# Feed-forward part of a decoder trunk: up products of two steps in turn, PSUM halves in turn in the down part, token sums in pieces, fewer products for the sample rows

## Chip, cores and metric

One Trainium2 chip, one of its cores. The metric is device time in microseconds (us) of one execution of the whole program; lower is better. PE is TensorE, DVE VectorE, ACT ScalarE, POOL GpSimd, SP SyncE, whose queue issues all the DMAs spoken of here.

## What is computed

The reference is a decoder layer (a mixer, then a squared-ReLU MLP) over 2048 prompt tokens and 8 sample tokens, in float32. The change touches only the MLP and the last norm:

```
x = x + ffn(rmsnorm(x, norm_ffn_g), w_up, w_down)      # x: 2048 + 8 rows of 1024
def ffn(h, w_up, w_down):                              # w_up 1024 x 4096, w_down 4096 x 1024
    return square(relu(h @ w_up)) @ w_down
y = rmsnorm(x, norm_f_g)
```

## The kernel before

The program projects, mixes (until about 1018 us of the profile) and then runs `ffn` (L1806), the only part that differs. Every matrix product is split by Strassen's scheme in Winograd's form: a 2x2 block product is made of 7 products k = 0..6 of sums of quarters. Each operand of a product is split in a high and a low part (`..._cut`, index 0 and 1), and `three_pass` (L114) issues three matmuls for each pair of 128-row pieces: L119, L120, L121.

**Up part.** 48 steps u (3 token blocks of 688 columns, 16 pairs of weight column blocks each), 7 products a step. A product is 4 pieces x 3 passes = 12 matmuls of 128x344. `SEQ` (L1762) is the order of all 336 products (a position in it is a tick); from step 2 on it is step by step, k = 0..6. `product(u, k)` on PE accumulates k = 0, 2, 4, 6 in `bank_a(u)` and k = 1, 3, 5 in `bank_b(u)`; three pairs of banks go round with u. Since a bank goes on being used, its sum so far has to be read out between products: k = 2 waits for ACT's copy of k = 0 (`copy_part`, L2256), k = 3 for DVE's `sum_part` of k = 1 (L2415), k = 4 for the copy of k = 2, k = 5 for the copy of k = 3, k = 6 for the sum of k = 4. `square_z` (ACT, L2263 and L2267) makes relu and square into `z`, which `store_z` (SP) writes to DRAM, both halves behind each other.

Weights: SP's `load_up(u)` brings 1 MB into one of two rooms `up_raw`; POOL's `sum_up(u)` makes four sums (L2091, L2093, L2096, L2100) into `wsum`; ACT cuts the high part (`w_cut_hi`, L2218), DVE the low one (`w_cut_lo`, L2375). Both run `LEAD` = 4 ticks ahead of PE and write `wc[:, k]`, one room for each k. The order on ACT at a tick is: cut of tick + 4, then the copy or the square of this tick, then what belongs to a turn or a block; on DVE: cut of tick + 4, `sum_part`, `scale_later`, `move_later`, `h_cut_lo`.

Tokens: the first block is turned at the start. The other rows are turned during the first steps: at 12 ticks `TURN_AT` (16 + 5i) PE transposes 128 rows (L2539), which DVE has scaled two ticks before (`scale_later`, L2409), and ACT and DVE move them out for a store. At the last step of a block (`u % PAIRS == 15`) `h_cut_hi` and `h_cut_lo` (L2236, L2379) cut the next block's tokens; POOL has made that block's four sums before, all in one go (`sum_h`, L2110; 128x1376 each), behind `sum_up(12)` and `sum_up(20)`, waiting for the block's load (`load_h`, L1967).

**Down part.** 16 chunks m of tokens and weight group g = m // 2, 7 products k each, `down(m, k)`. A product is 4 column pieces j x 2 x 3 = 24 matmuls of 128x512 into 4 banks: banks 0..3 for even k, 4..7 for odd k (`dbank`). DVE adds them into `acc` in two halves (`add`, L2441, 128x1024). `A_BEFORE`, `B_BEFORE` give the product whose adds a product waits for. ACT and DVE cut chunk parts (`z_cut_hi`, `z_cut_lo` L2420) two products ahead, and the weights of the next group over 7 products around each odd-to-even chunk change (`dn_cut_lo`, L2424); POOL makes the sums (L2131 to L2166). After each even chunk `sample(g)` multiplies the 8 sample rows: 10 pairs of a 32-column and a 64-column stationary operand, 128x512 each (L2605, L2607).

## Time and profile before

| | us |
|---|---|
| time before, median of 3 runs | 2510.64 (2510.34 to 2511.41) |
| the profiled execution, its own time | 2505.51 |
| its span, first to last instruction | 2503.8 |
| PE busy | 2337.5 (93%) |
| PE weight load busy | 2120.9 (85%) |
| DVE busy | 1622.3 (65%) |
| ACT busy | 986.6 (39%) |
| POOL busy | 796.4 (32%) |
| share of PE in the chain that ended last | 38% |

The profile is one execution. The page gives busy time by engine, a strip of 40 slices with the clock granted to TensorE, the chain of work that ended last, and the costliest groups of instructions. The end of a matmul is modelled, so PE's busy share says little; the distance from one matmul's start to the next one's says more. An idle time in square brackets stands in front of the instruction that ended it, with what released it.

### The profile page before, as it was taken

How to read it: one execution, taken by the hardware profiler on the slowest of the kernel's cores; microseconds unless marked ns; L12 is line 12 of the kernel's file. 1: busy time of each engine (PE TensorE's matmuls, PEld its weight loads, DVE VectorE, ACT ScalarE, POOL GpSimd, SP SyncE). 2: the span in 40 equal slices, each digit the busy share in tenths (PEclk: the TensorE clock that was granted, in tenths of full speed). 3: DMA queues.
4: the chain of work that ended last, by engine and by line, in shares of the span. 5: the costliest groups of instructions: out<-in, count | busy, mean ns of one | idle time of the engine just before them, and what ended most of it. 6: DMA issues, size and time to landing. Idle time of an engine off the chain costs nothing.

```text
span 2503.8 us, 34076 instructions
## 1 busy us (share of the span) xinstructions
PE 2337.5 (93%) x12740; PEld 2120.9 (85%) x12740; DVE 1622.3 (65%) x2317; ACT 986.6 (39%) x1959; POOL 796.4 (32%) x639
## 2 busy tenths in 40 slices
PE   7999999999999999688978999899899999999996
PEld 5999999999888887588978898899887778777874
DVE  6445664596766666766546656555677877787777
ACT  5323332211444443455546556665522222222233
POOL 4000011000233333343353543334534342434232
PEclk9999999999799999799989999999999999999998
DMA  5113334323754443365534433363452212221203
GB/s 172 49 53 108 111 113 126 117 76 112 231 152 145 146 144 118 93 201 180 166 103 140 131 118 121 101 201 120 152 180 76 93 42 85 85 84 46 91 26 135
DMA packets 303304, 296.72 MB, mean 119 GB/s; under 512 B 40460, under 2 KB 242544, under 8 KB 299804
## 3 DMA queue, kind: packets, MB, share of 16 engines
q1 hardware_dynamic: 303140, 294.54, 37.4%
q8 instruction: 102, 1.67, 0.3%
q14 instruction: 62, 0.51, 0.1%
HBM read 205.15 MB, written 89.44 MB: 118 GB/s over the span
## 4 chain that ended last, share of the span: by engine, by line
PE 38%; DVE 12%; ACT 4%; issue 4%; DMA 1%; POOL 0%; ACTq 0%; SPq 0%; DVEq 0%
PE bank L119 12%; PE bank L120 12%; PE bank L121 12%; DVE f_up_cut L2375 5%; ACT f_up_cut L2218 2%; DVE f_acc L2441 1%; DVE f_part L2415 1%; ACT f_part L2263 1%; DVE f_dn_cut L2424 1%; DVE f_z_cut L2420 1%; PE bank L2605 1%; PE bank L2607 1%; PE bank L2539 1%; DVE f_h_cut L2379 1%; DVE xn L2409 1%
## 5 line engine op out<-in xcount | busy, mean ns | idle before, releaser
L119 PE MATMUL bank<-f_h_cut,f_up_cut 128*128 128x344 f32 x1344 | 449.5, 334 | 74.2 <-ACT f_part L2256 34.5
L120 PE MATMUL bank<-f_h_cut,f_up_cut 128*128 128x344 f32 x1344 | 440.8, 328 | 0.0
L121 PE MATMUL bank<-f_h_cut,f_up_cut 128*128 128x344 f32 x1344 | 438.2, 326 | 0.0
L119 PE MATMUL bank<-f_dn_cut,f_z_cut 128*128 128x512 f32 x896 | 353.1, 394 | 17.4 <-DVE f_acc L2441 16.2
L2441 DVE TENSOR_TENSOR f_acc<-bank,f_acc 128x1024 f32<-128x1024 f32 x224 | 271.1, 1219 | 145.3 <-PE bank L121 145.2
L120 PE MATMUL bank<-f_dn_cut,f_z_cut 128*128 128x512 f32 x896 | 352.3, 393 | 0.0
L121 PE MATMUL bank<-f_dn_cut,f_z_cut 128*128 128x512 f32 x896 | 352.2, 393 | 0.0
L119 PEld LDWEIGHTS bank<-f_h_cut,f_up_cut 128*128 128x128 f32 x1344 | 260.8, 194 | 90.8 <-DVE f_up_cut L2375 46.3
L119 PE MATMUL bank<-h_hi,w_lo 128*128 128x412 f32 (+1 forms) x960 | 337.1, 351 | 0.0
L120 PE MATMUL bank<-h_lo,w_hi 128*128 128x412 f32 (+1 forms) x960 | 336.3, 350 | 0.0
L121 PE MATMUL bank<-h_hi,w_hi 128*128 128x412 f32 (+1 forms) x960 | 336.1, 350 | 0.0
L2375 DVE TENSOR_TENSOR f_up_cut<-f_up_sum,f_up_cut 128x512 fp32r<-128x512 f32 x192 | 201.3, 1063 | 192.5 <-ACT f_up_cut L2218 192.5
L120 PEld LDWEIGHTS bank<-f_h_cut,f_up_cut 128*128 128x128 f32 x1344 | 260.9, 194 | 0.0
L121 PEld LDWEIGHTS bank<-f_h_cut,f_up_cut 128*128 128x128 f32 x1344 | 260.8, 194 | 0.0
L119 PEld LDWEIGHTS bank<-f_dn_cut,f_z_cut 128*128 128x128 f32 x896 | 170.1, 190 | 56.4 <-issue 20.4
L121 PEld LDWEIGHTS bank<-f_dn_cut,f_z_cut 128*128 128x128 f32 x896 | 170.2, 190 | 36.0
L120 PEld LDWEIGHTS bank<-f_dn_cut,f_z_cut 128*128 128x128 f32 x896 | 170.2, 190 | 35.5
L2263 ACT ACTIVATE f_part<-f_part 128x344 f32<-128x344 f32 x144 | 70.8, 491 | 282.3 <-DVE f_part L2415 282.3
L120 PEld LDWEIGHTS bank<-h_lo,w_hi 128*128 128x128 f32 x960 | 181.0, 189 | 0.6
L119 PEld LDWEIGHTS bank<-h_hi,w_lo 128*128 128x128 f32 x960 | 181.1, 189 | 0.5
L121 PEld LDWEIGHTS bank<-h_hi,w_hi 128*128 128x128 f32 x960 | 181.1, 189 | 0.3
L2282 ACT ACTIVATE f_z_cut<-xn 128x1024 fp32r<-128x1024 f32 x68 | 72.2, 1063 | 249.4 <-PE bank L121 249.4
(443 smaller groups left out, 4101.9 us busy)
## 6 DMA issues: line engine op xcount, KB each, us to landing
z_dram<-f_z SPq DMA_DIRECT2D x96, 344.0 KB, 2.2
p_dram<-ffn_gains SPq DMA_DIRECT2D x24, 1024.0 KB, 4.6
up_raw<-in_w_up_dram SPq DMA_DIRECT2D x48, 512.0 KB, 5.0
f_up_raw<-in_w_up_dram SPq DMA_DIRECT2D x48, 512.0 KB, 5.4
xn<-z_dram SPq DMA_DIRECT2D x44, 512.0 KB, 3.7
f_dn_raw<-in_w_down_dram SPq DMA_DIRECT2D x32, 512.0 KB, 6.5
up_raw<-in_w_in_dram SPq DMA_DIRECT2D x24, 512.0 KB, 5.7
up_raw<-p_dram SPq DMA_DIRECT2D x48, 256.0 KB, 5.2
```

Source lines behind the costliest of these rows:

```text
L119: pe.matmul(out, wl, xh, start=start and k == 0, stop=False, skip_group_check=skip)
L120: pe.matmul(out, wh, xl, start=False, stop=False, skip_group_check=skip)
L121: last = pe.matmul(out, wh, xh, start=False, stop=stop and k == n - 1, skip_group_check=skip)
L2218: act.activation(wc[:, k, 0], w_source(u, k), ACT.Copy).then_inc(s["w_hi"], 1)
L2263: act.activation(part_of(k), bank_a(u) if k == 6 else part_of(k), ACT.Relu).then_inc(s["relued"], 1)
L2282: act.activation(ring[tick % 3][:, 0], z_source(m, k), ACT.Copy).then_inc(s["z_hi"], 1)
L2375: dve.tensor_tensor(wc[:, k, 1], w_source(u, k), wc[:, k, 0].bitcast(F32), ALU.subtract).then_inc(s["w_lo"], 1)
L2379: dve.tensor_tensor(hc[:, k, 1], h_source(k), hc[:, k, 0].bitcast(F32), ALU.subtract).then_inc(s["h_lo"], 1)
L2409: dve.scalar_tensor_tensor(out=out, in0=out, scalar=c.x1_rs[:, LATER[i]:LATER[i] + 1], in1=gain, op0=ALU.mult, op1=ALU.mult).then_inc(s["r ...
L2415: dve.tensor_tensor(part_of(k), bank_a(u) if k == 4 else bank_b(u), part_of(k), ALU.add).then_inc(s["summed"], 1)
L2420: dve.tensor_tensor(cut[:, 1], z_source(m, k), cut[:, 0].bitcast(F32), ALU.subtract).then_inc(s["z_lo"], 1)
L2441: dve.tensor_tensor(dst, heads(pair_of(k, jj), 2), dst, ALU.add).then_inc(s["y_added"], 1)
```

## The change

Only `ffn` and the constants before it change.

1. `SEQ` is sorted by a place: product k of step u has place 7u + 2k (steps 0 and 1 have places of their own). So products of two successive steps alternate: (u,0) (u-1,4) (u,1) (u-1,5) (u,2) (u-1,6) (u,3). `wc` becomes a ring over the tick (`at % K7`). ACT makes `square_z` one tick later, ahead of the copy of its tick. The first block's token cuts come in the order 0, 1, 3, 2, 4, 5, 6.
2. The quarter of the weights that k = 6 reads raw has three rooms of its own (`a22`, one of them the room of the last norm's gain, whose load moves behind the up part) and a load of its own (`load_a22`); `load_up(u + 2)` waits for other cuts. `store_z` is made of two calls with a semaphore for each half.
3. Turns come every 4 ticks instead of 5.
4. `sum_h` is cut into eight pieces of half the length, issued one or two behind each of `sum_up(11)` to `sum_up(15)` for the second block, one behind each of `sum_up(19)` to `sum_up(26)` for the third; the load of the second block stands one step earlier.
5. Down part: the half of PSUM is `4 * ((m + (k in B_KS)) % 2)`, so halves alternate also from chunk to chunk, and (m, 0) and (m, 1) wait for the adds of (m - 1, 5) and (m - 1, 6).
6. `sample(g)`: POOL makes two small sums (`sum_zs`) and PE issues 8 pairs instead of 10, in banks 6 and 7; DVE's `add_sample` comes first at its tick. At the end of the up part `square_z` of the last product stands behind two cuts on ACT.

```diff
-SEQ = [(0, 0), (0, 1), (1, 0), (1, 1)] + [(0, k) for k in range(2, K7)] + [(1, k) for k in range(2, K7)] \
-    + [(u, k) for u in range(2, STEPS) for k in range(K7)]
+def place(x):
+    u, k = x
+    if u == 0:
+        return (0, 2, 6, 4, 8, 10, 12)[k]
+    if u == 1:
+        return (2.4, 2.7, 11, 13, 15, 17, 19)[k]
+    return 7 * u + 2 * k
+SEQ = sorted(itertools.product(range(STEPS), range(K7)), key=place)
+H_FIRST = (0, 1, 3, 2, 4, 5, 6)
-TURN_AT = {16 + 5 * i: i for i in range(len(LATER))}
+TURN_AT = {16 + 4 * i: i for i in range(len(LATER))}
+T_SUMS_AT = {1: {11: (0, 1), 12: (2, 3), 13: (4, 5), 14: (6,), 15: (7,)}, 2: {PAIRS + 3 + x: (x,) for x in range(8)}}
-A_BEFORE = {0: (-1, 6), 2: (0, 0), 4: (0, 2), 6: (0, 4)}
-B_BEFORE = {1: (-1, 5), 3: (0, 1), 5: (0, 3)}
+A_BEFORE = {0: (-1, 5), 2: (0, 0), 4: (0, 2), 6: (0, 4)}
+B_BEFORE = {1: (-1, 6), 3: (0, 1), 5: (0, 3)}
...
+    a22 = [up_raw[0][:, 1, 4:8, :], up_raw[1][:, 1, 4:8, :], heads(c.gain_room[:, D:D + 512])]
...
-    dbank = lambda k, j: psum[(0 if k in A_KS else 4) + j][:, :]
+    first_bank = lambda m, k: 4 * ((m + (k in B_KS)) % 2)
+    dbank = lambda m, k, j: psum[first_bank(m, k) + j][:, :]
...
             for u in range(2, STEPS):
                 sum_up(u)
-                if u in (12, PAIRS + 4):
-                    sum_h(1 + u // PAIRS)
+                for x in T_SUMS_AT.get(1 + u // PAIRS, {}).get(u, ()):
+                    sum_h(1 + u // PAIRS, x)
...
-                if u:
-                    act.wait_ge(s["done"], AT[(u - 1, k)] + 1)
-                act.activation(wc[:, k, 0], w_source(u, k), ACT.Copy).then_inc(s["w_hi"], 1)
+                if at >= K7:
+                    act.wait_ge(s["done"], at - K7 + 1)
+                act.activation(wc[:, at % K7, 0], w_source(u, k), ACT.Copy).then_inc(s["w_hi"], 1)
...
+                if tick and SEQ[tick - 1] in SQUARED:
+                    square_z(*SEQ[tick - 1])
                 if k in (0, 2, 3):
                     copy_part(u, k)
-                else:
-                    square_z(u, k)
...
+            dn_cut_hi(0, 1)
             z_cut_hi(0, 1)
+            square_z(*SEQ[-1])
...
+                    if m % 2 and k == 0 and j >= 2:
+                        pe.wait_ge(s["s_added"], 2 * (m // 2) + j - 1)
...
-                for d, parts in enumerate((((0, 0), (1, 1)), ((3, 0), (0, 0), (5, 1)))):
-                    pairs = [(k, q, 2 * q + a) for q in range(2) for k, a in parts]
-                    bank = psum[4 + d]
+                for d in range(2):
+                    pairs = [(k, q, f) for q in range(2) for k, f in (((5, 4 + q), (4, 6 + q)) if d else ((0, 2 * q), (1, 2 * q + 1)))]
+                    bank = psum[6 + d]
```

## Rows read from the trace of the kernel before

**Rows 1.** The page: busy time by engine, share of the span, instructions.

```profile
PE 2337.5 (93%) x12740; PEld 2120.9 (85%) x12740; DVE 1622.3 (65%) x2317; ACT 986.6 (39%) x1959; POOL 796.4 (32%) x639
```

**Rows 2.** Stages: length, busy us of PE, PEld, DVE, ACT, POOL, clock, DMA, GB/s.

```profile
1028.00:1082.00 54.00, 39.22 (x208) 38.05 (x208) 39.58 (x37) 26.70 (x49) 29.62 (x39) 0.81 0.27 92
1304.00:1346.00 42.00, 31.87 (x175) 30.28 (x174) 27.02 (x28) 26.55 (x46) 14.03 (x9) 0.88 0.28 90
...
1592.00:1782.00 190.00, 182.60 (x1129) 177.68 (x1128) 107.78 (x136) 113.58 (x242) 81.62 (x57) 1.00 0.45 145
```

**Rows 3.** Groups of instructions, 1028 to 1805: busy, mean ns, idle before, releasers.

```profile
L119 PE MATMUL bank<-f_h_cut,f_up_cut 128*128 128x344 f32 x1344 | 449.5, 334 | 74.2 <-ACT f_part L2256 34.5 <-DVE f_part L2415 32.0 <-DVE f_up_cut L2375 5.0
...
L2539 PE MATMUL bank<-ident,xn 128*128 128x128 f32 x88 | 11.7, 276 | 15.5 <-DVE xn L2409 15.4
```

**Rows 4.** PE's matmuls around one ordinary step, in order of time.

```profile
1363.65 0.39 PE L119 MATMUL bank<-f_h_cut,f_up_cut 128*128 128x344 f32 x1 [0.53 <-DVE f_part L2415]
...
1376.94 0.32 PE L121 MATMUL bank<-f_h_cut,f_up_cut 128*128 128x344 f32 x1
1377.78 0.40 PE L119 MATMUL bank<-f_h_cut,f_up_cut 128*128 128x344 f32 x1 [0.52 <-DVE f_part L2415]
...
1378.17 0.32 PE L121 MATMUL bank<-f_h_cut,f_up_cut 128*128 128x344 f32 x1
...
1379.59 0.32 PE L121 MATMUL bank<-f_h_cut,f_up_cut 128*128 128x344 f32 x1
```

**Rows 5.** DVE in the same stretch.

```profile
1374.27 2.93 DVE L2375 TENSOR_TENSOR f_up_cut<-f_up_sum,f_up_cut 128x512 fp32r<-128x512 f32 x2 [0.76 <-ACT f_up_cut L2218]
1377.13 0.50 DVE L2415 TENSOR_TENSOR f_part<-bank,f_part 128x344 f32<-128x344 f32 x1
...
1380.15 7.19 DVE L2375 TENSOR_TENSOR f_up_cut<-up_raw,f_up_cut 128x512 fp32r<-128x512 f32 x2
```

**Rows 6.** POOL in the same stretch.

```profile
1375.04 1.62 POOL L2093 TENSOR_TENSOR f_up_sum<-f_up_sum,up_raw 128x512 f32<-128x512 f32 x1
...
1380.14 3.17 POOL L2114 TENSOR_TENSOR xn<-f_h_raw 128x1376 f32<-128x1376 f32 x1 [0.55 <-DMA f_h_raw<-hT_dram]
```

**Rows 7.** PE in order of time: the longest wait of the up part.

```profile
1276.15 0.63 PE L119 MATMUL bank<-f_h_cut,f_up_cut 128*128 128x344 f32 x1 [12.91 <-ACT f_part L2256]
```

**Rows 8.** POOL in order of time before that wait.

```profile
1255.02 3.49 POOL L2114 TENSOR_TENSOR xn<-f_h_raw 128x1376 f32<-128x1376 f32 x1 [14.97 <-DMA f_h_raw<-hT_dram]
```

**Rows 9.** PE in order of time around one turn.

```profile
1204.80 1.06 PE L2539 MATMUL bank<-ident,xn 128*128 128x128 f32 x8 [2.00 <-DVE xn L2409]
1205.62 0.40 PE L119 MATMUL bank<-f_h_cut,f_up_cut 128*128 128x344 f32 x1
```

**Rows 10.** PE in order of time: where two samples of the down part begin.

```profile
1928.08 0.39 PE L2607 MATMUL bank<-f_dn_cut,f_zs 128*64 128x512 f32 x1
...
2013.05 0.39 PE L2607 MATMUL bank<-f_dn_cut,f_zs 128*64 128x512 f32 x1
```

**Rows 11.** PE in order of time at one odd-to-even chunk change.

```profile
1973.27 0.47 PE L119 MATMUL bank<-f_dn_cut,f_z_cut 128*128 128x512 f32 x1 [2.29 <-DVE f_acc L2441]
```

**Rows 12.** The stretch just behind it, in the columns of rows 2.

```profile
1974.00:1977.00 3.00, 3.00 (x8) 2.32 (x8) 2.52 (x3) 0.00 (x0) 0.23 (x1) 0.50 0.15 16
```

**Rows 13.** DVE in order of time over that change.

```profile
1964.04 3.42 DVE L2424 TENSOR_TENSOR f_dn_cut<-f_dn_raw,f_dn_cut 128x1024 fp32r<-128x1024 f32 x1
1967.38 2.34 DVE L2441 TENSOR_TENSOR f_acc<-bank,f_acc 128x1024 f32<-128x1024 f32 x2
...
1971.92 2.34 DVE L2441 TENSOR_TENSOR f_acc<-bank,f_acc 128x1024 f32<-128x1024 f32 x2
```

**Rows 14.** PE in order of time at the seam of up part and down part.

```profile
1806.40 0.47 PE L119 MATMUL bank<-f_dn_cut,f_z_cut 128*128 128x512 f32 x1 [1.22 <-ACT f_z L2267]
```

**Rows 15.** ACT in order of time there.

```profile
1806.16 1.99 ACT L2282 ACTIVATE f_z_cut<-xn 128x1024 fp32r<-128x1024 f32 x2
```

**Rows 16.** The page: issues of the weight load, KB each, median us to landing.

```profile
f_up_raw<-in_w_up_dram SPq DMA_DIRECT2D x48, 512.0 KB, 5.4
```

## What I expect of the change

> **What bounds the kernel now.** I read the busy times first, then the stages, then the groups of PE with the idle time in front of them, then PE in order of time. PE is busy 93% of the span and no other engine is near it [rows 1], so the question is how much of PE's time is its own work, and what it waits for in the rest. Everything before 1028 us is untouched.
>
> PE's own work in the up part: within a product a matmul starts every (1379.59 - 1378.17) / 9 = 0.158 us [rows 4]. With 12 matmuls a product takes 1.90 us, a step 13.3, all 336 products 639. They take from 1028.5 to 1805.0, 776.5 us. The 12 turns need (0.82 us of transposes each [rows 9]) some 11 with the early ones. So about 126 us are lost. Of these 89.7 are idle time [rows 3], 74.2 and 15.5; the rest, 36, is the restart after each wait and matmuls at the lower of the two clocks (1.2 instead of 2.4 GHz) behind long waits: the mean granted clock is 0.81 at the start and 0.88 around a block change [rows 2].
>
> The idle time is never in front of a weight that came late from DRAM. It is in front of a product that needs DVE's sum or ACT's copy of an earlier product of the same step, or of a turn whose rows DVE has scaled late [rows 3]. In an ordinary step this is one wait: (u,3) needs the sum of (u,1), and only (u,2), 1.9 us, lies between. DVE has two low cuts ahead of that sum; they take 2.93 us together instead of 1.3, since each waits for a POOL sum [rows 5, 6]. PE waits 0.52 us and loses 1377.78 - 1376.94 - 0.16 = 0.68; the period is 1377.78 - 1363.65 = 14.13 against 13.3 [rows 4].
>
> **The loss of the up part by place.** (a) Start, 1028.5 to 1081.8: 16 products, 30.4 us of work, 53.3 of time, 23 lost. (b) 12 turns over 137 us with 55 products (104.6): 33 lost, of which 9 are transposes. (c) The second block's token sums: POOL does four sums of 3.2 to 3.5 us in one go after 15.0 us of waiting for the load [rows 8], the next weight sums queue behind, ACT's cut behind them, a copy behind that: 13.2 lost [rows 7]. The third block's hold DVE: two low cuts take 7.19 us beside them [rows 5, 6], 5 lost. (d) Two block changes: 42 us with 14.6 products' work [rows 2] (175 matmuls / 12), 14 lost each. Ordinary steps cost DVE 107.78 / 190 x 14.1 = 8.0 us and ACT 8.4 [rows 2]; in the 42 us, 2.1 steps' work, DVE has 27.0 - 16.8 = 10 us more and ACT 26.6 - 17.6 = 9 more: the 7 token cuts. (e) About 30 ordinary steps at 0.8: 24. (f) The last steps, where cuts of the down part come on top: 7. Sum 133 with the 9 of (b), against 126 + 11: the remaining 4 are small.
>
> **What the change does to each.**
> Alternating the steps (edit 1) puts at least one foreign product more in each chain. Between (u,1) and (u,3) stand (u-1,5), (u,2), (u-1,6): 5.7 us instead of 1.9, and the same 5.7 for each other pair. The late square costs one tick of ACT, nobody on PE waits for it soon (the bank of step u comes back at u + 3). Per step ACT and DVE do the same, about 8 us of 13.3. So (e) goes to about nothing; what hides the sums is the 5.7 us, and if DVE fell 5 us behind, it would come back. I leave 4 for (e) and small losses.
> (d): a block's last step is now spread over 14 ticks, not 7, so the 10 us of token cuts meet 26.6 us of PE time with 16 of other DVE work: 26, just full, and ACT the same (9 on 17). Going through the ticks by hand with undisturbed durations, every operand is ready 0.8 to 1.3 us before PE wants it; with POOL in between it will not always be. From nothing to 7 each; I take 4, together 8 instead of 28.
> (c): a piece has half the length, 1.6 us, and stands between two weight sums. POOL waits for the third block's load in front of `sum_up(20)`: the load is issued behind the store of (17,6), 13 us (as from issue to the first sum before) is 7 ticks, so tile 1 of step 20 is ready 3.6 us after ACT would take it. ACT then delays cuts that are 4 ticks, 7.6 us, ahead. No loss on PE; 18 saved.
> (b): the transposes stay. Scaling is done two ticks ahead, behind ACT's cut and, in 5 of 12 cases, behind a `sum_part`. Before, a step's first tick was worst, since the square of (u-1,6) stood in front on ACT; that is gone. DVE's scale, 1024 columns as an add, takes 1.2 us undisturbed [rows 13] and ends 1.75 us after that product, where PE needs it at 1.9; with a POOL sum in the way it is 1 late. 5 x 1 to 1.3 plus 12 x 0.25 for going over to transposes, plus some restarts: 11, and 9 of transposes, 20 instead of 33. The denser turns (every 4th tick) add 1.9 us of DVE per 7.6 and fit.
> (a): (0,3) comes before (0,2), as its token sum does, and ACT makes token cuts ahead of squares that it used to wait for. The order of the first sums on DVE and POOL, which hold each other, stays, and so does the low clock. I take two ticks' time, 4 us, from none to 8: 19 instead of 23.
> (f): the last four products still follow each other: 8.
> Sum of losses after: 19 + 20 + 0 + 8 + 4 + 8 = 59 instead of 137.5 (transposes in both): **78.5 us less**.
> Weights (edit 2): SP's queue now has three waits more a step, with stores in between. `load_up(u+2)` can go when the sums of step u are made, about tick 7u + 1, and lands 5.4 us later [rows 16]; POOL wants it at 7u + 9. Cover about 9 us. Price nothing. The gain's load is needed only at the end.
> **Seam.** PE waits 1.22 us for the last square [rows 14]; now one weight cut and one chunk cut stand ahead of it on ACT. Two chunk cuts take 1.99 [rows 15], the weight cut falls mostly in the last product: 1.5 us worse (1 to 2).
>
> **Down part.** Period of two chunks 2013.05 - 1928.08 = 84.97 us [rows 10]. At each odd-to-even change (7 of them) the first product waits for the adds of the product right before it, in the same half: idle 2.29 us [rows 11], 2.5 with the restart. DVE is late since a low cut takes 3.42 us beside POOL [rows 13]. Behind it the clock granted falls to 0.50 [rows 12] in this case; 3 us at half the clock cost 1.6, and I take 5 of the 7 cases, 8 (0 to 11). With alternating halves (4,0) waits for (3,5), added from 1967.38 on and half ready at 1968.5, its second half at 1969.7; PE wants them at 1970.8 (1973.27 less 2.46 of delay [rows 11]) and half a product later, 1973.5 [rows 13]. (4,1) wants (3,6)'s, ready 1973.1 and 1974.3, at 1976.2 and 1978.9. So all 7 waits go: 7 x 2.5 = 17.5, and the low clock behind them 8. What is next late is DVE itself, with 4.8 us of 5.4 a product there; margin about 1 us at the tightest.
> Sample: 20 matmuls become 16, at (84.97 - 2.5 - 1.6) / 356 = 0.227 us: 0.9 x 8 = 7.3. DVE's `add_sample` must be ready when PE reaches the third column piece of the next product, 2.7 us after the sample's end; the first of two 0.7 us adds can begin when half the sample is done. Two POOL sums over 8 columns cost under 0.5 us of POOL, off the path. Sum **33 us less**.
>
> **Total.** -78.5 + 1.5 - 33 = -110. The profiled execution took 2505.5 (span 2503.8 and 1.7 around), 5.1 below the median of 2510.6: 2395.5 for such a one, **2400.6** against the median.
>
> **A rule of the skill.** A low cut beside POOL takes 3.6 us (7.19 for two) while POOL's two sums run 3.17 us and more [rows 5, 6]. The Trainium skill (SBUF — State Buffer, section Who interferes with whom) says that a DVE instruction with two SBUF inputs contends with a GpSimd one that reads SBUF, and that the one that comes second is blocked for the whole of the other. By this rule the eight pieces hold DVE in total as long as four whole sums did; only each hold is shorter. It would speak against saving at the block changes, where DVE is full; it is rival A.
>
> **Rivals.**
> A. DVE and ACT, no longer given air by PE's waits, fall behind by more than the 5.7 us. For: the block change is full by my count. Against: 8 of 13.3 us in ordinary steps. Price: ordinary steps keep 0.4 of 0.8 (12 - 4 = 8), block changes 11 each instead of 4 (14), turns as before (9): 31 more, 2432.
> B. More gain: POOL's sums are now spread over a step, not in one burst, so turns and block changes lose nothing: 8 + 8 less, start 3 less: 2382.
> C. The change doesn't do what it says in the down part: DVE is late at (4,1) or the sample instead. Price: 17.5 + 8 kept: 2426. Against: 3 us of margin at (4,1).
> D. Slower than before: SP. Its queue holds `load_a22(u+3)`, `load_up(u+2)` and two stores, each with a wait; if the weights of every step came late, each of 46 steps would stretch. It needs 110 / 46 = 2.4 us a step above a cover of 9, a landing 11 to 12 us after the issue is due, where it is 5.4 [rows 16], with DMA at 0.27 to 0.45 of its time [rows 2]. At 3 us a step: 46 x 3 - 110 = 28 more than before, 2538.
>
> **How the numbers follow.** Forecast 0.70 (2400, from 2386 to 2416 by the ends of (b), (d) and the seam), A 0.15, B 0.07, C 0.05, D 0.015, something near no change 0.015. Faster 0.97. A difference of 0.2% (5 us) is what a measurement of this kernel can tell. For 8 in 10 the range reaches into B and to A: 2382 to 2434.
>
> **What would show it.** PE of the up part: period of a step 13.3 (14.1 means the chain is still there); no wait above 2 us after 1060 except at block changes; idle before L119 well under 30 us instead of 74. Down part: period 80.0; no DVE wait at the chunk change, clock 1.00 throughout. The start still loses about 19. Wrong would be the prediction above all if waits for `f_up_cut` or the copies grew in every step.

## The result, and the profile after

The changed kernel takes **2379.28 us** (median of 3 runs, 2378.51 to 2379.32) against 2510.64: a ratio of 0.9475 (0.9454 to 0.9497), 131 us less. I forecast 2400, so the gain was 21 us larger than my sum, and the time lies 3 us below the low end of my range. One run of experiment 7, 2616 us at a clock of 0.84 where its others have 0.98, is left out of its median. The profiled execution of the changed kernel took 2378.51 us, 127.0 less than the profiled one of the kernel before (2505.51); its span is 2376.8. From here on a line number of the changed kernel is one or some forty higher: the matmuls of `three_pass` are L120 to L122, the low cut of a weight L2416, the sum L2456, ACT's high cut L2258, its copy L2296, its square L2303 and L2307.

The page after, busy time by engine, answers to [rows 1]: PE has 32 matmuls less, those of the samples, and its share is 97% instead of 93%.

```profile
PE 2297.5 (97%) x12708; PEld 2100.6 (88%) x12708; DVE 1587.5 (67%) x2317; ACT 1003.3 (42%) x1959; POOL 779.8 (33%) x663
```

The groups of PE in the up part after, in the columns of [rows 3]: idle time before a product 16.4 us instead of 74.2, before a turn 2.0 instead of 15.5.

```profile
L120 PE MATMUL bank<-f_h_cut,f_up_cut 128*128 128x344 f32 x1344 | 438.1, 326 | 16.4 <-DVE f_up_cut L2416 6.7 <-DVE f_h_cut L2420 6.4 <-DVE f_part L2456 3.0
...
L2580 PE MATMUL bank<-ident,xn 128*128 128x128 f32 (+1 forms) x96 | 12.2, 268 | 2.0 <-DVE xn L2450 1.9
```

Stages after, in the columns of [rows 2]: the start, the first block change, twelve ordinary steps. The first is little better (clock 0.84, before 0.81), the second runs at full clock (before 0.88), and in the third PE never stops while DVE has 73.84 / 160 x 13.3 = 6.1 us of work a step, where it had 8.0.

```profile
1028.00:1082.00 54.00, 41.33 (x217) 40.07 (x217) 43.88 (x41) 28.77 (x52) 33.41 (x41) 0.84 0.37 116
1264.00:1306.00 42.00, 41.16 (x256) 40.05 (x255) 33.62 (x37) 34.60 (x65) 18.25 (x14) 1.00 0.45 141
1520.00:1680.00 160.00, 160.00 (x1012) 160.00 (x1011) 73.84 (x121) 107.48 (x218) 65.75 (x49) 1.00 0.48 156
```

PE's waits after, in order of time (start in us, duration, what it is, in brackets the idle time and what ended it): three of the start, the longest at a turn, two of the first block change, the last two products, and the seam (the place where the down part begins), which answers to [rows 14]. The 12.91 us wait of [rows 7] has no successor.

```profile
1041.08 0.66 PE L120 MATMUL bank<-f_h_cut,f_up_cut 128*128 128x344 f32 x1 [5.07 <-DVE f_up_cut L2416]
1050.43 0.63 PE L120 MATMUL bank<-f_h_cut,f_up_cut 128*128 128x344 f32 x1 [2.58 <-DVE f_part L2456]
1059.29 0.39 PE L120 MATMUL bank<-f_h_cut,f_up_cut 128*128 128x344 f32 x1 [3.31 <-DVE f_h_cut L2420]
...
1081.14 1.06 PE L2580 MATMUL bank<-ident,xn 128*128 128x128 f32 x8 [1.09 <-DVE xn L2450]
...
1274.11 0.43 PE L120 MATMUL bank<-f_h_cut,f_up_cut 128*128 128x344 f32 x1 [0.34 <-DVE f_up_cut L2416]
1286.48 0.43 PE L120 MATMUL bank<-f_h_cut,f_up_cut 128*128 128x344 f32 x1 [0.50 <-DVE f_up_cut L2416]
...
1701.39 0.40 PE L120 MATMUL bank<-f_h_cut,f_up_cut 128*128 128x344 f32 x1 [0.33 <-ACT f_part L2296]
1703.94 0.39 PE L120 MATMUL bank<-f_h_cut,f_up_cut 128*128 128x344 f32 x1 [0.41 <-DVE f_part L2456]
1708.82 0.47 PE L120 MATMUL bank<-f_dn_cut,f_z_cut 128*128 128x512 f32 x1 [2.77 <-ACT f_z L2307]
```

The up part runs from 1028.6 to 1705.9, 677.3 us instead of 776.5: **99 us less**, where my terms gave 78.5. The down part, from the seam to its last matmul, takes 643.1 us instead of 672.5: **29 less** for 33. With 1.5 more at the seam that is the 127 of the two profiled executions; the other 4 of the 131 come from the medians, since the profiled execution of before lies 5.1 below its own and that of after 0.8. The period of two chunks, the distance of two samples' begins, is 80.24 us, answering to [rows 10]:

```profile
1828.94 0.39 PE L2648 MATMUL bank<-f_dn_cut,f_zs 128*64 128x512 f32 x1
```

(The next but one begins at 1989.44.) DVE over an odd-to-even chunk change of the changed kernel, as [rows 13]: the adds are later relative to the product than before, since a small cut stands in front, yet PE stops for some 0.27 us only: it comes to that product at 1951.0, when the first of the two adds is about done. The clock is 1.00 at all seven changes.

```profile
1944.21 3.42 DVE L2465 TENSOR_TENSOR f_dn_cut<-f_dn_raw,f_dn_cut 128x1024 fp32r<-128x1024 f32 x1
1947.56 2.42 DVE L2469 TENSOR_TENSOR f_zs<-f_zs_raw,f_zs 128x64 fp32r<-128x64 f32 x1
1949.90 2.34 DVE L2482 TENSOR_TENSOR f_acc<-bank,f_acc 128x1024 f32<-128x1024 f32 x2
```

### The profile page after: what moved, and what is told of

Same layout as the page of the kernel before. It is cut to its first block, busy times and chain, and to the rows that moved or that the text cites. A ratio compares the mean times of both kernels' runs of the same rounds, so it can differ in the third digit from the quotient of the medians.

```text
span 2376.8 us, 34154 instructions
## 1 busy us (share of the span) xinstructions
PE 2297.5 (97%) x12708; PEld 2100.6 (88%) x12708; DVE 1587.5 (67%) x2317; ACT 1003.3 (42%) x1959; POOL 779.8 (33%) x663
## 4 chain that ended last, share of the span: by engine, by line
PE 50%; DVE 4%; ACT 1%; issue 1%; POOL 1%; DVEq 0%; ACTq 0%; POOLq 0%
PE bank L120 16%; PE bank L121 16%; PE bank L122 16%; DVE f_h_cut L2420 1%; PE bank L2580 1%; DVE f_up_cut L2416 1%; PE bank L2646 1%; PE bank L2648 1%; ACT f_h_cut L2276 1%; DVE f_acc L2491 1%; DVE f_part L2456 0%; DVE f_acc L2482 0%; ACT f_part L2303 0%; DVE xn L2450 0%; DVE xn L2516 0%
## 5 line engine op out<-in xcount | busy, mean ns | idle before, releaser
L120 PE MATMUL bank<-f_h_cut,f_up_cut 128*128 128x344 f32 x1344 | 438.1, 326 | 16.4 <-DVE f_up_cut L2416 6.7
L121 PE MATMUL bank<-f_h_cut,f_up_cut 128*128 128x344 f32 x1344 | 434.0, 323 | 0.0
L122 PE MATMUL bank<-f_h_cut,f_up_cut 128*128 128x344 f32 x1344 | 431.2, 321 | 0.0
L120 PE MATMUL bank<-f_dn_cut,f_z_cut 128*128 128x512 f32 x896 | 349.8, 390 | 3.6 <-ACT f_z L2307 2.8
L122 PE MATMUL bank<-f_dn_cut,f_z_cut 128*128 128x512 f32 x896 | 349.4, 390 | 0.0
L120 PE MATMUL bank<-h_hi,w_lo 128*128 128x412 f32 (+1 forms) x960 | 337.3, 351 | 0.0
L122 PE MATMUL bank<-h_hi,w_hi 128*128 128x412 f32 (+1 forms) x960 | 336.1, 350 | 0.0
L120 PEld LDWEIGHTS bank<-f_h_cut,f_up_cut 128*128 128x128 f32 x1344 | 255.0, 190 | 20.4 <-DVE f_up_cut L2416 12.8
L122 PEld LDWEIGHTS bank<-f_h_cut,f_up_cut 128*128 128x128 f32 x1344 | 255.1, 190 | 0.0
L121 PEld LDWEIGHTS bank<-f_h_cut,f_up_cut 128*128 128x128 f32 x1344 | 254.6, 189 | 0.0
L2416 DVE TENSOR_TENSOR f_up_cut<-f_up_sum,f_up_cut 128x512 fp32r<-128x512 f32 x192 | 151.1, 788 | 98.5 <-ACT f_up_cut L2258 98.2
L120 PEld LDWEIGHTS bank<-f_dn_cut,f_z_cut 128*128 128x128 f32 x896 | 168.6, 188 | 42.0 <-issue 6.6
L122 PEld LDWEIGHTS bank<-f_dn_cut,f_z_cut 128*128 128x128 f32 x896 | 168.6, 188 | 35.2
L120 PEld LDWEIGHTS bank<-h_hi,w_lo 128*128 128x128 f32 x960 | 181.4, 189 | 0.5
L122 PEld LDWEIGHTS bank<-h_hi,w_hi 128*128 128x128 f32 x960 | 181.1, 189 | 0.4
L420 POOL TENSOR_TENSOR xn<-xn,ga 128x512 f32<-128x512 f32 x16 | 16.7, 1043 | 353.6 <-DMA xn<-g_dram 353.6
```

Source lines behind the costliest of these rows:

```text
L120: pe.matmul(out, wl, xh, start=start and k == 0, stop=False, skip_group_check=skip)
L121: pe.matmul(out, wh, xl, start=False, stop=False, skip_group_check=skip)
L122: last = pe.matmul(out, wh, xh, start=False, stop=stop and k == n - 1, skip_group_check=skip)
L2416: dve.tensor_tensor(wc[:, at % K7, 1], w_source(u, k), wc[:, at % K7, 0].bitcast(F32), ALU.subtract).then_inc(s["w_lo"], 1)
```

## The experiments

What had to be told apart: **theory 1**, that of the prediction, says that the alternation of two steps lets PE run on, by its 5.7 us between a product and its reader. **Theory 2** came from the traces: the place of `square_z`, a relu and a square on ACT, in ACT's queue made a loop. "The square" stands for both instructions below. Here is ACT in an ordinary step before (start, duration, operation). It has cut three weights by 1375.1, then stops at the square of the sum of k = 1 until 1377.66, with the next cut queued behind it.

```profile
1372.17 0.62 ACT L2218 ACTIVATE f_up_cut<-f_up_sum 128x512 fp32r<-128x512 f32 x1
...
1373.62 0.62 ACT L2218 ACTIVATE f_up_cut<-f_up_sum 128x512 fp32r<-128x512 f32 x1
1374.14 0.44 ACT L2256 ACTIVATE f_part<-bank 128x344 f32<-128x344 f32 x1
1374.48 0.62 ACT L2218 ACTIVATE f_up_cut<-f_up_sum 128x512 fp32r<-128x512 f32 x1
1377.66 0.49 ACT L2263 ACTIVATE f_part<-f_part 128x344 f32<-128x344 f32 x1 [2.56 <-DVE f_part L2415]
```

That sum stands on DVE behind two low cuts, which came together because ACT had made the high ones together, and which took 2.93 us beside POOL's sum [rows 5, 6]. So ACT waits for DVE's sum, DVE's next cut for ACT's, and the cuts come in bunches right ahead of the next sum. In one group of the trace of before, ACT's squares of sums, the wait is 282 us long:

```profile
L2263 ACT ACTIVATE f_part<-f_part 128x344 f32<-128x344 f32 x144 | 70.8, 491 | 282.3 <-DVE f_part L2415 282.3
```

After, ACT cuts first one and then the next weight, and the square finds its sum after 0.3 us, in one case of three after 1.0:

```profile
1598.20 0.62 ACT L2258 ACTIVATE f_up_cut<-f_up_raw 128x512 fp32r<-128x512 f32 x1
1599.12 0.49 ACT L2303 ACTIVATE f_part<-f_part 128x344 f32<-128x344 f32 x1 [0.30 <-DVE f_part L2456]
...
1600.10 0.62 ACT L2258 ACTIVATE f_up_cut<-f_up_sum 128x512 fp32r<-128x512 f32 x1
```

All times below are medians of at least three runs. No experiment edits anything ahead of the up part, yet in the traces it begins anywhere from 1026.5 to 1031.4 us. So a difference of a few us between medians (1, 3, 4, 12, 13) says little by itself, and the length of the edited part in the trace is given beside it.

**1. The order alone put back** (of the changed kernel, products step by step).

```diff
-    return 7 * u + 2 * k
+    return 7 * u + k
-        return (2.4, 2.7, 11, 13, 15, 17, 19)[k]
+        return (2.4, 2.7, 12.1, 12.2, 12.3, 12.4, 12.5)[k]
```

> The changed kernel (2379.3 us) with one thing undone: the products stand step by step again from step 1 on, all else as changed (square a tick late, weight rooms, pieces, turns every 4 ticks). Theory 1, the alternation is what took the waits of the up part away: ordinary steps go back to a period of 14.1 us (30 steps x 0.8 = 24), each of the two block changes to 13 us of loss instead of about 2 (22), turns to some 10 more, together 50 to 65 slower than the changed kernel, 2429 to 2444. Rival, it was POOL's sums being spread over the step and cut in pieces that freed DVE: within 10 us of the changed kernel.

2385.85 us, only 6.6 slower than the changed kernel; its up part takes 686.5 us instead of 677.4, 9 more. Its ordinary steps have no wait; four of 0.7 to 1.7 us stand at the first block change, where the changed kernel has two of 0.3 and 0.5. Theory 1 falls as an account of most of the gain.

**2. The old halves of PSUM.**

```diff
-    first_bank = lambda m, k: 4 * ((m + (k in B_KS)) % 2)
+    first_bank = lambda m, k: 4 * (k in B_KS)
```

(with `A_BEFORE`, `B_BEFORE` and one wait as before)

> The changed kernel with PSUM halves in the down part as before (banks 0 to 3 for even k, 4 to 7 for odd k, waits for the adds accordingly). Theory 1: 7 waits of 2.3 us with a restart come back, with the half clock behind most of them: 17.5 + 5 to 8, so 2402 to 2405. Rival, DVE is late at the chunk change anyway and the alternation only moved the wait: under 8 us slower.

2425.31: 46 slower, twice the expected. The wait at a chunk change is longer than in the kernel before, 4.63 us instead of 2.29 [rows 11], and the granted clock is 0.63 and 0.80 in the two stretches of 3 us from its end on:

```profile
1970.42 0.47 PE L120 MATMUL bank<-f_dn_cut,f_z_cut 128*128 128x512 f32 x1 [4.63 <-DVE f_acc L2482]
```

By the trace the reason is the small cut of 2.42 us shown above: it stands right ahead of those adds here too, and the wait is 2.34 longer. In the kernel before it stood elsewhere and took 0.18. No run moves that cut alone. The clock fell behind all seven waits. In the kernel before it fell behind five of its seven, to 0.53 to 0.72 over the next 3 us, and stayed at 1.00 behind the two others, though all seven waits are 2.3 or 2.4 us long; where it fell, two products took 12.4 instead of 10.8 us, 1.6 more. So the waits cost about 7 x 2.45 + 5 x 1.6 = 25 us in the kernel before and would cost 46 in the changed one (7 x 4.5, and 14 by the clock).

**3. Ten pairs for the sample again.** The two lines of `pairs` as before.

> The changed kernel with 10 pairs of products a sample group instead of 8. Theory 1: 4 matmuls of 0.227 us more in each of 8 groups, all on PE's path: 7.3 us, 2386.6. Rival, the sample's matmuls fill time in which PE would wait for adds: no difference.

2385.22, 5.9 slower for the 7.3 of the sum. In the trace the period of two chunks is 81.18 instead of 80.23 us, 7.6 in eight groups.

**4. The token sums in one go again.**

```diff
-T_SUMS_AT = {1: {11: (0, 1), 12: (2, 3), 13: (4, 5), 14: (6,), 15: (7,)}, 2: {PAIRS + 3 + x: (x,) for x in range(8)}}
+T_SUMS_AT = {1: {12: range(8)}, 2: {PAIRS + 4: range(8)}}
```

> The changed kernel with the eight half token sums of a block in one go again, behind the weight sums of steps 12 and 20. Theory 1, the alternating order has 5.7 us between a copy or a sum and its product, so POOL's 13 us block is mostly absorbed: 0 to 6 us slower. Rival (the step of my sum that gave the pieces 18 us of their own): 14 to 20 us slower, 2393 to 2399.

2376.07 (2374.59 to 2379.66): no difference; the up part takes 678.1 us instead of 677.4. The 18 us that I put down to the pieces are gone by something else. One thing this run leaves as changed is the load of the second block, which is issued one step earlier. POOL never waits for it here, where in the kernel before it waited 14.97 us [rows 8]. The kernel before with the late square alone (5) has the late load too, and the long wait is still there:

```profile
1226.92 3.46 POOL L2114 TENSOR_TENSOR xn<-f_h_raw 128x1376 f32<-128x1376 f32 x1 [14.67 <-DMA f_h_raw<-hT_dram]
...
1247.90 0.63 PE L119 MATMUL bank<-f_h_cut,f_up_cut 128*128 128x344 f32 x1 [10.46 <-ACT f_part L2256]
```

It is gone in every run with the early load (in 7 too, with order and square as before). So the load's place is the likeliest cause; it was not tested alone.

**5. The kernel before, with the late square alone.**

```diff
+                if tick and SEQ[tick - 1] in SQUARED:
+                    square_z(*SEQ[tick - 1])
                 if k in (0, 2, 3):
                     copy_part(u, k)
-                else:
-                    square_z(u, k)
...
+            square_z(*SEQ[-1])
             z_cut_hi(0, 1)
```

> The kernel before with one edit of ACT's queue alone: the relu and square of a product is issued one tick later, behind the weight cut of the next tick instead of ahead of it. Theory 2, formed after the run with the old order of the products lost only 7 us: in the kernel before ACT stands waiting for DVE's sum with the next weight cut queued behind it, so DVE's cuts bunch up in front of the next sum; the late square breaks that loop. Then the 0.8 us of an ordinary step go (24) and most of the turns' waits (12), part of the block changes: 35 to 55 us faster than before, 2455 to 2475. Theory 1 (only the alternation gives the slack): within 8 us of the kernel before.

2434.84: **75.8 us less** than before (ratio 0.9701, 0.9685 to 0.9717), more than the 35 to 55 expected, by moving one call behind one cut. Ordinary steps take 13.3 us and lose nothing, and the up part takes 707.3 us instead of 776.7. ACT's wait of 282 is halved, PE's idle time before a product goes from 74.2 to 39.9:

```profile
L119 PE MATMUL bank<-f_h_cut,f_up_cut 128*128 128x344 f32 x1342 | 438.7, 327 | 39.9 <-ACT f_part L2256 20.1 <-DVE f_part L2416 14.8 <-DVE f_up_cut L2376 5.1
...
L2263 ACT ACTIVATE f_part<-f_part 128x344 f32<-128x344 f32 x144 | 70.8, 492 | 138.2 <-DVE f_part L2416 138.1
```

**6. The changed kernel with the square back at its own tick**, the alternation kept (the diff of 5 reversed, except that the last square stays behind the loop).

> The changed kernel with the square back at its own tick, ahead of the next tick's weight cut; the products still alternate. Theory 2 says either of the two edits is enough in ordinary steps, as the alternation gives each sum 5.7 us: 0 to 10 us slower than the changed kernel (block changes and turns). If the late square alone did it, 25 us or more slower.

2455.0, **75.7 us more** than the changed kernel, where I expected 10 at most. The groups of its up part show the loop again:

```profile
L120 PE MATMUL bank<-f_h_cut,f_up_cut 128*128 128x344 f32 x1336 | 446.6, 334 | 49.5 <-DVE f_up_cut L2416 28.2 <-ACT f_part L2296 9.8 <-DVE f_part L2456 8.8
...
L2303 ACT ACTIVATE f_part<-f_part 128x344 f32<-128x344 f32 x142 | 69.9, 492 | 257.5 <-DVE f_part L2456 257.5
L2580 PE MATMUL bank<-ident,xn 128*128 128x128 f32 (+1 forms) x96 | 14.7, 302 | 16.8 <-DVE xn L2450 14.3 <-DVE xn L2444 2.3
```

The turns wait 16.8 us again too: DVE's scaling stands behind the bunched cuts. The first row also shows what the alternation does and doesn't do. The waits for sums and copies are 19 us where [rows 3] have 66.5, as its 5.7 us promised, but those for low cuts have grown from 5.0 to 28.2. As I read the rows, a cut comes out of the same loop, and a foreign product between two others gives it no distance. So ordinary steps still take 13.9 us, 0.6 lost of the 0.8 before, with such a wait:

```profile
1387.80 0.42 PE L120 MATMUL bank<-f_h_cut,f_up_cut 128*128 128x344 f32 x1 [0.78 <-DVE f_up_cut L2416]
```

**7. Both put back**, order and square (the diffs of 1 and of 6).

> The changed kernel with both undone, products step by step and the square at its own tick; weight rooms, pieces, denser turns and the whole down part as changed. Theory 2: the waits of the kernel before come back, 24 in ordinary steps, 20 at block changes, 10 to 15 at turns: 2430 to 2445. Rival, the weight rooms, SP's new order or the pieces took part of them away: under 2415.

2470.48 (2470.34 to 2472.19), 91.2 more than the changed kernel; I expected 50 to 65. Its up part takes 771.5 us: the two edits together are 94 of the 99 us that the up part gained. With 1, 6 and the changed kernel all four combinations are measured: the late square is worth 75.7 with the alternation and 84.6 without it, the alternation 6.6 with the late square and 15.5 without.

**8. The kernel before, with small sums on POOL.** From step 1 on each of the four weight sums is made over 2 instead of 128 columns.

```diff
-                tile = lambda i: heads(wsum[:, i, :])
+                cols = slice(0, P if u == 0 else 2)
+                tile = lambda i: heads(wsum[:, i, :])[:, :, cols]
```

> The kernel before with POOL's four weight sums of a step made over 2 instead of 128 columns of each piece from step 1 on (so that part of the computation is left out; every instruction and wait stays). Theory of the prediction, POOL's sums hold DVE's low cuts and so make the sum late: DVE's two cuts ahead of the sum take 1.3 instead of 2.9 us, the ordinary wait goes, 25 to 35 us faster than before. If ACT's queue alone makes them late: under 10 us.

2459.0, 51.7 less than before, again more than expected. This run leaves the weight sums out almost wholly, and nothing else. In ordinary steps a low cut takes 0.72 us on average instead of 0.97, and the steps lose nothing; but ACT's wait is still 223 of 282 us long:

```profile
L2265 ACT ACTIVATE f_part<-f_part 128x344 f32<-128x344 f32 x144 | 70.8, 492 | 223.2 <-DVE f_part L2417 223.2
```

So PE's wait in an ordinary step of the kernel before needed both, the square ahead of the cut and POOL's sums; without either it is gone (5, 8). The length of ACT's wait is thus no measure of what it costs PE. How much of the 51.7 is the hold on DVE and how much is that the sums themselves are ready sooner, this run doesn't tell.

**9. The changed kernel with small sums on POOL.** The same edit.

> The changed kernel, in which POOL makes the four weight sums of each step from step 1 on over 2 instead of 128 columns of each head, so most of the sums' values are left out and the output is not the reference's. The same edit took 51.7 us off the kernel before. Theory 2: POOL's hold on DVE lengthened a loop that the late square has broken, so it is hidden now: 0 to -5 (2374 to 2380), all of it at the start and the block changes. The rival, that POOL's sums are a cost of their own: a third or more of the 51.7 remains, 2360 or less.

2368.99, 10.3 less, between the two expectations. In its trace 6.7 of it lie in the up part: some 1.3 at the start, 1.8 at the turns (no wait in front of any), 3.6 around the two block changes (none there either). So four fifths of what POOL cost is hidden now; what it still costs stands where DVE is fullest.

**10. Each low cut twice.** DVE's cover, measured in the alternating order and step by step.

```diff
+                dve.tensor_tensor(wc[:, at % K7, 1], w_source(u, k), wc[:, at % K7, 0].bitcast(F32), ALU.subtract).then_inc(s["dup"], 1)
+                dve.wait_ge(s["dup"], at + 1)
                 dve.tensor_tensor(wc[:, at % K7, 1], w_source(u, k), wc[:, at % K7, 0].bitcast(F32), ALU.subtract).then_inc(s["w_lo"], 1)
```

> The changed kernel, in which DVE makes each low cut of a weight piece twice (same result, the second behind the first), 336 more instructions of 128x512, 0.70 us each: 4.8 us of DVE more in a step, 235 us in all. It measures how much lateness the changed kernel can take. Theory 2 (the late square removed the wait loop; the alternation is spare cover): DVE has 6.1 us of work in an ordinary step of 13.3, so it becomes 11 and still fits, the 5.7 us between a product and its reader hide the rest; ordinary steps show no wait; only the block changes and turns, where DVE is full, pay, 5 to 10 us each of the two changes and some at the turns: 2390 to 2410. The rival, that DVE stands at the edge already (rival A of the prediction): each cut's 0.7 us shows up in at least one wait a step, 48 x 0.7 = 34 or more: 2415 to 2450.

> The same doubled cut, in the changed kernel with products step by step. There only one product, 1.9 us, lies between k = 1 and k = 3, and between k = 4 and k = 6, and DVE must do two cuts and a sum in that time: 2 x 1.4 + 0.5 = 3.3 us, or 1.4 + 0.5 = 1.9 where one cut is in front. Theory 2 (the alternation is cover that was not needed as the changed kernel stands): the cover is missing now; two waits of 0.5 to 1.4 us in each step, 45 steps x 1 to 2.5: 2430 to 2500, at least 30 above the alternating one. The rival, that the distance does not matter once the square is late: the doubled cut costs both orders the same, and this kernel stays 7 us above the alternating one.

2516.2 and 2514.48: 137 us more than the changed kernel, above all that I expected (up to 2410, and up to 2500 step by step), and the same in both orders. The stretch of ordinary steps shows why (columns of [rows 2]): DVE is busy 148 of 160 us.

```profile
1520.00:1680.00 160.00, 142.98 (x849) 133.09 (x847) 148.18 (x179) 94.67 (x188) 61.35 (x41) 1.00 0.35 113
```

PE makes 849 / 84 = 10.1 steps in it, 15.8 us a step instead of 13.3. DVE has 14.7 us a step. Its own are 14 cuts x 0.69 + 3 sums x 0.51 = 11.2; the other 3.5 are holds, about 0.9 for each of POOL's four sums. Here is one (DVE's cut starts 0.56 us after POOL's sum and lasts until 0.55 after its end, 1.66 instead of 0.68):

```profile
1612.33 0.68 DVE L2416 TENSOR_TENSOR f_up_cut<-f_up_sum,f_up_cut 128x512 fp32r<-128x512 f32 x1
1613.05 1.66 DVE L2418 TENSOR_TENSOR f_up_cut<-f_up_sum,f_up_cut 128x512 fp32r<-128x512 f32 x1
...
1612.49 1.67 POOL L2130 TENSOR_TENSOR f_up_sum<-f_up_raw,f_up_sum 128x512 f32<-128x512 f32 x1 [3.46 <-DVE f_up_cut L2418]
```

My expectation added up DVE's own work and left the holds out of it. With DVE as the bound, the order of products tells nothing of the alternation.

**11. The low cuts of k = 1, 3 and 5 alone twice**, in both orders.

> The changed kernel, in which DVE makes the low cut of a weight piece twice for the products k = 1, 3 and 5 alone: three more instructions of 0.7 us a step, 2.1 us. With all seven doubled both orders took 2515, and DVE was busy 148 of 160 us: it had become the bound, and the order no longer mattered. With three, DVE has 6.1 + 2.1 us of its own in 13.3, and up to 4 more where POOL's sums hold it. Theory 2 (the alternation is cover the changed kernel hardly uses): it hides the three: ordinary steps show no wait, turns and block changes a little: 2380 to 2392.

> The same in the changed kernel with products step by step, which took 2385.9. The low cuts ahead of the sums of k = 1, 4 and 6 on DVE are those of k = 5, 1 and 3, the doubled ones. If the distance of one product (1.9 us) was nearly used up before, each sum is now up to 0.7 us late: 45 steps x 0.7 to 2: 2415 to 2475, and the alternation is worth 30 to 80 where DVE is loaded more. If a loop through ACT was all that ever made PE wait, both orders take the doubled cuts alike and the difference stays 6 to 10: 2386 to 2400.

2393.5 alternating, 2450.85 step by step: 14 and 65 us more than without the extra cuts. Step by step every ordinary step waits again:

```profile
1608.01 0.39 PE L120 MATMUL bank<-f_h_cut,f_up_cut 128*128 128x344 f32 x1 [0.78 <-DVE f_part L2461]
1622.33 0.39 PE L120 MATMUL bank<-f_h_cut,f_up_cut 128*128 128x344 f32 x1 [0.79 <-DVE f_part L2461]
```

The period is 14.32. Alternating, PE has no gap in 140 us, though DVE's work has grown by 4.1 us a step (107.55 / 140 x 13.3 = 10.2 against 6.1); 2.1 are the three cuts, and 2.0 are cuts that take longer beside POOL than before:

```profile
1540.00:1680.00 140.00, 140.00 (x886) 140.00 (x885) 107.55 (x140) 94.49 (x192) 56.75 (x43) 1.00 0.50 163
```

So the 5.7 us of theory 1 are real. As the changed kernel stands, they are spare cover.

**12. The cuts of dn (0,1) back at k = 3 of the last step.**

```diff
+                if u == STEPS - 1 and k == 3:
+                    dn_cut_hi(0, 1)
-            dn_cut_hi(0, 1)
```

(and the same for `dn_cut_lo`)

> The changed kernel with the high and low cut of the weight piece dn (0,1) back at the tick of the last step's k = 3, where they stood before, ahead of the last copies on ACT. It prices term (f) of the prediction, 8 us for the last steps, where the changed kernel loses 1. If the place of these cuts made that loss, it comes back in part: 1 to 4 us more, 2380 to 2383, and the last square comes 1 us earlier, which takes a part of it away at the seam. If the loss hung on the square and its loop, no difference.

2382.16 (2380.54 to 2384.78), 2.9 more; the up part takes 681.6 us instead of 677.4. PE's wait before the last product is 3.72 us instead of 0.41, and 2.17 instead of 2.77 at the seam. The place of these cuts explains 3 to 4 of the 7 us by which term (f) was too high.

**13. The last square ahead of the two cuts at the seam.**

```diff
+            square_z(*SEQ[-1])
             dn_cut_hi(0, 1)
             z_cut_hi(0, 1)
-            square_z(*SEQ[-1])
```

> The changed kernel with the square of the last up product on ACT ahead of the last two high cuts instead of behind them, an attempt at a better kernel. In the trace of the changed kernel PE waits 2.77 us there, and its clock is at half for some 2 us behind. If the square's place makes that wait, about 1 us of cuts goes from in front of it: 1.2 to 1.5 us of wait remain and less of the low clock: -1.5 to -3, 2376 to 2378. If the z cut that PE needs next is now what is late, the wait is only renamed: no difference.

2373.88 (2373.26 to 2375.47), 5.4 less than the changed kernel and below both kernels (ratio to before 0.9463, 0.9449 to 0.9477; that interval overlaps the changed kernel's, the times don't). The wait is the 1.22 of [rows 14] again:

```profile
1706.26 0.47 PE L120 MATMUL bank<-f_dn_cut,f_z_cut 128*128 128x512 f32 x1 [1.22 <-ACT f_z L2307]
```

The down part begins 2.56 us earlier (1708.82 - 1706.26): 1.55 by the wait, 0.28 by the up part, and 0.74 because the up part began earlier, which the edit can't have done. Another 1.6 is the clock: the down part takes 641.5 us instead of 643.1. In the changed kernel the row behind the seam is (the last but two numbers of a row are shares: granted clock, then DMA)

```profile
1708.00:1710.00 2.00, 1.18 (x4) 0.97 (x5) 2.00 (x2) 1.91 (x4) 0.00 (x0) 0.80 1.00 287
1710.00:1712.00 2.00, 2.00 (x6) 1.58 (x5) 2.00 (x3) 0.57 (x1) 1.78 (x1) 0.50 0.99 363
1712.00:1714.00 2.00, 2.00 (x9) 1.59 (x8) 2.00 (x1) 0.00 (x0) 2.00 (x2) 0.85 0.99 344
```

and 1.00 from 1706 to 1712 in this run. But the long wait doesn't decide that. Twelve of the traces have the seam's wait of 2.75 to 2.80 us; behind it the clock fell in six and stayed at 1.00 in the other six, and each of these six has the down part of 641.5 us. Here is the row of experiment 4 behind its wait of 2.76 us:

```profile
1711.00:1714.00 3.00, 2.44 (x11) 2.03 (x12) 3.00 (x4) 2.32 (x3) 1.04 (x1) 1.00 0.98 337
```

So the place of the square is worth 1.55 us, and at times 1.6 more. The rest of the 5.4 is the scatter ahead of it: experiment 4, with the square where the changed kernel has it, has a run of 2374.59 too.

## Why the prediction was right or wrong

**The direction and the two parts** were right: PE was held by waits for sums and copies, the losses were 137.5 us in the up part, and most of them went. What made most of them go was not what I said.

**The step that failed** is the first of the change's: "Alternating the steps (edit 1) puts at least one foreign product more in each chain", with "the late square costs one tick of ACT, nobody on PE waits for it soon". I looked at who waits for the square and found nobody. I had to look at what stands queued behind it: the high cut of a weight, which DVE's low cut needs. And I counted the distance only between a product and the sum or copy of it, not for the cuts: with the alternation alone PE waits 28.2 us for low cuts, and an ordinary step loses 0.6 us, where I had said about nothing (6). The late square, which I priced at nothing, was the larger part of the edit (75.7 of its gain, 5, 6 and 7), and the alternation, to which I gave all, is worth 7 as the kernel stands. That the sum came out near is luck: the late square takes the ordinary steps' wait to nothing, which the sum credited to the alternation. It came out too small in part (11 of the 20 us that it missed in the up part, (b) and (d) below) because I left a lateness of DVE at turns and block changes in it that comes with the loop: it is back in 6.

**The terms of the up part**, forecast and measured (loss over PE's own 639 us; what is measured is the distance of matmul starts beyond the regular 0.158 us):

| term | before | forecast | after |
|---|---|---|---|
| (a) start | 23 | 19 | 20.9 |
| (b) turns, with 9 of transposes | 33 | 20 | 13.8 |
| (c) second and third block's token sums | 18 | 0 | 0 |
| (d) two block changes | 28 | 8 | 3.3 |
| (e) ordinary steps | 24 | 4 | 0 |
| (f) last steps | 7 | 8 | 1.1 |
| sum | 133 (137.5 with small ones) | 59 | 39 |

(b): I charged 5 turns 1 to 1.3 us each for DVE's scale and 3 us for going over to the transposes; three waits are there, 1.09, 0.52 and 0.25 us. (d): two waits of 0.3 and 0.5 us at each change instead of 4 us. Here my hand-made schedule with undisturbed durations, "every operand is ready 0.8 to 1.3 us before PE wants it", was nearly right, and the 4 added for POOL were not needed. (f): carried over from before, and 1 more without a reason given, because "the last four products still follow each other", though the change moves the cuts that stood between them; that is 3 to 4 of the 7 (12), and the cause of the rest is open. (c): right in the sum, but not by the pieces (4); the earlier load of the second block, to which I gave nothing, is the likeliest cause, and not shown.

**The seam**: +1.5 forecast, 2.77 - 1.22 = 1.55 measured. The term was right. The low clock behind it, 1.6 us in this execution, was not in the term; it comes in half of the traces with this wait (13).

**The down part**: the mechanism held in each point: no DVE wait worth the name at the chunk change, period 80.24 for the forecast 80.0. Of the 4 us that are missing 1.9 are eight periods times 0.24, and 1.6 the low clock at the seam. The low clock behind five of the seven chunk changes and its 8 us were right (2), and all seven changes run at 1.00 now. What I had not seen is that the change also makes DVE later there, by the small cut: without alternating halves the waits would cost 46 us instead of 25 (2).

**The weights** (rival D): the load lands 4.5 us after its issue, and no wait of PE leads to it. **Rival A**: DVE and ACT did not fall behind. By own work DVE had 7 us of 13.3 spare; experiment 10 shows that with the holds it was about 3 to 4. The Trainium skill (SBUF — State Buffer, section Who interferes with whom) says that a DVE instruction with two SBUF inputs contends with a GpSimd one that reads SBUF. The traces agree: 1.66 us for a cut of 0.68 in experiment 10, and in the changed kernel 2.42 for one of 128x64. What I drew from the rule, that POOL holds DVE in total as long as before, did not come: DVE's cuts in ordinary steps take 0.69 to 0.74 us after, against 0.74 to 1.10 before (the groups of L2416 and L2375 there), since ACT now hands them over one by one, mostly between POOL's sums. **Rival B** (2382) came nearest: turns and block changes lose almost nothing, as it said, and its start was 5 us too good. Its reason, POOL's sums spread over a step, isn't enough: with all else as changed and the square alone at its old tick (6) the two steps at each block change lose 13 to 15 us.

**Do the parts add up?** Late square -75.8 (5), halves -46 (2), alternation -6.6 (1), sample -5.9 (3), dn cuts -2.9 (12) and seam +5.4 (13) make -132 for -131.4, but this agreement is luck, since by place they don't fit. The halves and the sample are 52 of it, and the down part gained 29.4 in the traces: some 20 of the 46 only pay for the small cut's new place. The up part has 85 of it, and gained 99. What adds up is this: order and square together 91.2 (7), and from the kernel before to that run 40.2, of which 5.1 is the distance of the profiled execution of before from its median and the traces show 35.0. These are 29.4 in the down part, 5.2 in the up part, 1.9 ahead of it, where nothing was edited, and -1.6 at the seam. So the other edits of the up part are worth 5 us with the old order and the old square. With the late square they are worth more: from the kernel before with the late square (5) to the changed kernel step by step (1) the up part goes from 707.3 to 686.5 us, 10.5 of it by the long wait of the late load (4).

## What to carry to other kernels

For an instruction that waits on an in-order engine, price what is queued behind it and not only who reads its result; if that is work prepared ahead for another engine, put it first, and the wait second. Where two engines wait for each other in turn, a one-line move may do what a reordering of the whole work does; and a reordering that adds distance pays only as far as what it gives distance to is late (here the sums, not the cuts made ahead), so measure its cover by adding load before counting on it. An engine's load is its own work plus what other engines hold of it.

## What the hardware showed that I had not expected

A DVE cut of 128x64 took 2.42 us in the changed kernel. It began 0.87 us after a POOL sum of 3.20 us and ended 0.1 after it:

```profile
1946.69 3.20 POOL L2167 TENSOR_TENSOR xn<-up_raw,xn 128x1024 f32<-128x1024 f32 x1
```

(the cut is the row at 1947.56 above). How long a small DVE instruction takes here goes by what is left of POOL's, not by its own size; its place added 2.34 us to each of seven waits in experiment 2, and lower clock behind them. And the holds are no fixed tax: the same four sums of a step cost DVE next to nothing in the changed kernel (its 85 cuts between 1520 and 1680 average 0.71 us, an undisturbed one takes 0.68), 3.5 us when its cuts stand close together (10), and 1.9 before (8.0 - 6.1).

The same wait doesn't always cost the same. Of the twelve waits of 2.75 to 2.80 us at the seam six were followed by a low clock and six by 1.00, and of the seven waits of 2.3 or 2.4 us at the chunk changes of the kernel before five and two. A fall behind a wait of 2.3 to 2.8 us cost 1.6 us, at the seam in two traces of the six 2.8. In the four traces in which the seam's wait is 1.22 us the clock stayed at 1.00.
